# The order of latent and context columns at the two norms of a two-model Trainium2 kernel

## What is computed

```python
def _layer(x, ctx, ..., update_ctx):            # second model, called for l = 0 and l = 1
    hx = _rmsnorm(x, norm_g) * (1.0 + scale_x) + shift_x
    hc = _rmsnorm(ctx, norm_g) * (1.0 + scale_c) + shift_c
    px = hx @ w_in
    a_k, a_v, b_k, b_v, a_q, b_q, a_z, b_z, g_a, g_b = _split(px, SPLIT_SIZES)
    pc = hc @ (w_in if update_ctx else w_in[:, :KV_COLS])
    ...
    x_new = x + gate_x * out_x
    if update_ctx:                              # only for l = 0
        ctx = ctx + gate_c * out_c
    return x_new, ctx
```

## Time and profile before

| | |
|---|---|
| median of 3 runs | 2992.94 us (2992.8 to 2994.6) |
| the profiled execution: its time, its span | 2993.36 us, 2991.7 us |
| TensorE busy | 2904.7 us, 97% of the span |
| VectorE, ScalarE, GpSimd busy | 1041.1, 720.0, 232.8 us |
| TensorE's mean granted clock | 0.989 |

### The profile page before, as it was taken

One profiled execution on the slowest core, in us unless ns is written; L12 is line 12 of the kernel. 1 busy time (PEld: TensorE's weight loads), 2 busy tenths in 40 slices (PEclk: granted clock), 3 DMA queues, 4 the chain that ended last, 5 costly groups with the idle time before them and its releaser, 6 DMA issues.

```text
span 2991.7 us, 41281 instructions
## 1 busy us (share of the span) xinstructions
PE 2904.7 (97%) x16802; PEld 1686.2 (56%) x16802; DVE 1041.1 (35%) x2032; ACT 720.0 (24%) x1389; POOL 232.8 (8%) x296
## 2 busy tenths in 40 slices
PE   6899999999999999999998999999999899999998
PEld 2777777776444444444444567765555544775443
DVE  3455555553231234444312226521011312552011
ACT  3344444442200002212002226620000012462000
POOL 0222222220000000000000101000000001100000
PEclk9999999999999999999999999999999999999999
DMA  5111111103244433444321210001111122101222
GB/s 204 54 40 40 35 41 35 35 30 128 77 141 139 136 97 126 161 147 155 98 84 58 74 43 30 1 29 56 50 49 49 49 63 75 43 2 57 77 76 72
DMA packets 61301, 220.93 MB, mean 74 GB/s; under 512 B 6688, under 2 KB 8864, under 8 KB 60896
## 3 DMA queue, kind: packets, MB, share of 16 engines
q1 hardware_dynamic: 42512, 153.11, 16.2%
q0 software_dynamic: 14656, 56.93, 5.9%
q10 hardware_dynamic: 3984, 8.71, 0.8%
HBM read 215.01 MB, written 2.15 MB: 73 GB/s over the span
## 4 chain that ended last, share of the span: by engine, by line
PE 95%; DMA 1%; DVE 1%; ACT 1%; issue 1%; POOL 0%; DVEq 0%; ACTq 0%; POOLq 0%; SPq 0%
PE psum L366 92%; PE psum L735 3%; DMA arena<-in_ctxT 1%; DMA arena<-in_stream 0%; DMA arena<-in_mods 0%; PE psum L552 0%; DVE arena L1258 0%; ACT arena L923 0%; ACT arena L1043 0%; PE psum L505 0%; ACT arena L1146 0%; ACT arena L916 0%; DVE arena L1636 0%; ACT arena L910 0%; DVE arena L1650 0%
## 5 line engine op out<-in xcount | busy, mean ns | idle before, releaser
L366 PE MATMUL psum<-arena 64*64 64x64 f32 (+6 forms) x16002 | 2810.6, 359 | 74.2 <-ACT arena L923 15.7
L366 PEld LDWEIGHTS psum<-arena 128*128 128x128 f32 (+4 forms) x16002 | 1599.9, 161 | 1266.5 <-issue 1114.5
L1477 DVE SCALAR_TENSOR_TENSOR arena<-arena 128x1024 f32<-128x1024 f32 x128 | 149.2, 1220 | 5.1 <-DMA arena<-in_mods 4.8
L1730 DVE SCALAR_TENSOR_TENSOR arena<-arena,psum 128x512 f32<-128x512 f32 x32 | 21.2, 684 | 371.7 <-PE psum L366 371.7
L1146 ACT ACTIVATE arena<-psum,arena 128x512 f32<-128x512 f32 (+2 forms) x160 | 115.3, 728 | 31.2 <-DVE arena L1642 18.2
L1200 ACT ACTIVATE arena<-psum 128x512 f32<-128x512 f32 x32 | 19.1, 597 | 372.5 <-PE psum L366 372.5
L1604 DVE COPY arena<-psum 128x512 f32<-128x512 f32 x26 | 18.0, 692 | 238.8 <-PE psum L366 238.8
L735 PE MATMUL psum<-arena 128*128 128x128 f32 x704 | 94.2, 279 | 4.2 <-ACT arena L1146 4.0
L1821 POOL DMA_DIRECT2D arena<-in_bias x16 | 8.8, 552 | 1111.6 <-DVE arena L1614 849.6
L735 PEld LDWEIGHTS psum<-arena 128*128 128x128 f32 x704 | 76.3, 140 | 29.0 <-issue 14.8
L1815 POOL DMA_DIRECT2D arena<-in_mods x76 | 40.1, 528 | 670.0 <-DVE arena L1477 670.0
(11 more groups left out here) (206 smaller groups left out, 1340.5 us busy)
## 6 DMA issues: line engine op xcount, KB each, us to landing
arena<-in_stream SPq DMA_DIRECT2D x288, 512.0 KB, 3.6
arena<-in_mods POOLq DMA_DIRECT2D x80, 512.0 KB, 3.6
arena<-gc_rows POOLq DMA_DIRECT2D x16, 384.0 KB, 4.7
arena<-in_bias POOLq DMA_DIRECT2D x16, 384.0 KB, 3.9
arena<-in_xT ACTq DMA_DIRECT2D x1, 2048.0 KB, 18.2
out<-arena SPq DMA_DIRECT2D x1, 2048.0 KB, 7.2
arena<-in_conds ACTq DMA_DIRECT2D x1, 1536.0 KB
arena<-arena POOLq DMA_DIRECT2D x4, 384.0 KB, 4.3
```

The source lines that it names most:

```text
L366: return pe.matmul(out, lhsT, rhs, start=start, stop=stop, skip_group_check=True)
L1477: m = stt(mjunk[:, b % 2, :] if x < len(conds) - 1 else slot, slot, 0.5, cb[:, c, :], ALU.mult, ALU.mult, accum_out=dst(x))
```

## The change

Norm 2 and norm 4 are each split in two, the context's part ("2c", "4c") ahead of the latent's.

- The context's sum is a small product of its own (`ctx_norm_sum`, into bank 1). At layer 0 it stands in the middle of the down product, after its fourth output tile; at layer 1 in the middle of the last output tile of the out product, whose context products now come before its latent ones (this order holds for output tiles 3 and 7). VectorE scales the context's eight tiles before it adds the last latent tile.
- The value product is done in two passes over the same four weight tiles. The first does the two context chunks for all eight k, with the latent's sum after k = 2 (into bank 0); the second does the four latent chunks for all eight k. The context chunks stand in banks 2 and 3 and the latent chunks in 4 to 7 (`value_bank`). A weight tile counts as used after the second pass.
- Five loops of two rounds over the output tiles are written out as straight code (down product and out product on TensorE, their additions on VectorE), and the wait for `con2` stands behind the value product.

```diff
+ROOTS = {n: at + 1 for at, n in enumerate((0, 1, "2c", 2, 3, "4c", 4))}
+NORMED = {n: KT * at for at, n in enumerate((0, 1, "2c", 2, "4c", 4))}
...
+        def value_bank(c):
+
+            return 4 + c if c < XC else 2 + c - XC
+
...
+            def ctx_norm_sum(count):
+
+                pe.wait_ge(s("sqsum"), count)
+                mm(psum[:, 1, 0:CTX], ones, sqb[:, 1, SEQ:TOK]).then_inc(s("nsum"), 1)
+
...
-            with pe.Fori(0, 2) as i:
+            for i in range(2):
                 for j in range(4):
                     pe.wait_ge(s("xd"), 4 * i + j - 3 + 4)
                     for b in range(3):
                         kt = 8 if b < 2 else FT - 16
                         product(T_DOWN + 3 * j + b, G, 4 + j, None, i, 12, kt, 8 * b, b == 0, b == 2)
-            norm_sums(2, (0, 1), True)
+                if i == 0:
+                    ctx_norm_sum(SUMS[2] - KT)
...
+                def near_values(k, chunks, normed):
+
+                    w = weights(pe, T0 + L_VA + k // 2)
+                    pe.wait_ge(s("H"), normed + k + 1)
+                    for c in chunks:
+                        m = mm(psum[:, value_bank(c), :], H[:, k, c * P:(c + 1) * P],
+                               w[:, (k % 2) * NAW:(k % 2 + 1) * NAW], k == 0, k == KT - 1)
+                    if k % 2 and c < XC:
+                        m.then_inc(s("used"), 1)
+
+                for k in range(KT):
+                    near_values(k, range(XC, CH), NORMED["4c" if l else "2c"])
+                    if k == 2:
+                        pe.wait_ge(s("sqsum"), SUMS[4] + 1 if l else SUMS[2])
+                        mm(psum[:, 0, :], ones, sqb[:, 1, 0:SEQ]).then_inc(s("nsum"), 1)
+                for k in range(KT):
+                    near_values(k, range(XC), NORMED[4 if l else 2])
                 pe.wait_ge(s("b2load"), 16 * 2)
-                if l:
-                    norm_sums(4, (0, 1), True)
-                for q in range(4):
-                    w = weights(pe, T0 + L_VA + q)
-                    for kk in range(2):
-                        k = 2 * q + kk
-                        pe.wait_ge(s("H"), KT * (2 + l) + k + 1)
-                        for c in range(CH):
-                            m = mm(psum[:, 2 + c, :], H[:, k, c * P:(c + 1) * P], w[:, kk * NAW:(kk + 1) * NAW],
-                                   k == 0, k == KT - 1)
-                    m.then_inc(s("used"), 1)
...
+                        w = weights(pe, T0 + L_OUT + j, i, 4)
+                        for k in range(KT):
+                            m = mm(psum[:, slot2(j)[1], 0:CTX], w[:, k * P:(k + 1) * P], MG2[:, k, SEQ:TOK],
+                                   k == 0, k == KT - 1)
+                        m.then_inc(s("out_ctx"), 1)
+                        for k in range(KT):
+                            m = mm(psum[:, slot2(j)[0], 0:SEQ], w[:, k * P:(k + 1) * P], MG2[:, k, 0:SEQ],
+                                   k == 0, k == KT - 1)
+                            if i and k == 2:
+                                ctx_norm_sum(SUMS[4])
+                        m.then_inc(s("used"), 1)
...
+            norm_root("2c", ((SEQ, TOK, 1),))
+            norm_shift(NORMED["2c"], ((SEQ, TOK, 1),), adaT[:, 0:8, :])
             act.wait_ge(s("xd"), 8 + 4)
             act.dma_start(con2, a_con2).then_inc(s("b2load"), 16)
-            norm_root(2, (0, 1), True, eps=vec("eps", 5))
+            norm_root(2, ((0, SEQ, 0),), eps=vec("eps", 5))
...
+                    norm_root("4c", ((SEQ, TOK, 1),))
+                    norm_shift(NORMED["4c"], ((SEQ, TOK, 1),), adaT[:, 24:32, :])
+                    norm_root(4, ((0, SEQ, 0),))
+                norm_shift(NORMED[4 if l else 2], ((0, SEQ, 0),), adaT[:, 24 * l:24 * l + 8, :])
...
+                if i == 0:
+                    dve.wait_ge(s("gmod"), 4)
+                    norm_scale("2c", ((SEQ, TOK, 1),))
...
+                    for k in range(KT - 1):
+                        dve.wait_ge(s("used"), T0 + L_OUT + k + 1)
+                        for q in range(2):
+                            add_out(k, q)
+                        dve.wait_ge(s("b2_xo"), 2 * k + 2 + 8)
+                        squares_add(4, k, TOK)
+                    dve.wait_ge(s("out_ctx"), 2)
+                    add_out(KT - 1, 1)
+                    last_squares(1, SEQ, TOK)
+                    norm_scale("4c", ((SEQ, TOK, 1),))
+                    dve.wait_ge(s("used"), T0 + L_OUT + KT)
+                    add_out(KT - 1, 0)
+                    last_squares(2, 0, SEQ)
```

More of the change, by code:

```diff
@@ L891, in _ @@
                 pe.wait_ge(s("b2_tg"), 16 * l + 2 * KT + FREE)
-                with pe.Fori(0, 2) as i:
+                for i in range(2):
                     for j in range(4):
                         pe.wait_ge(s("b2_xo"), 16 * l + (2 - l) * (4 * i + j - 3) + 8)
-                        product(T0 + L_OUT + j, MG2, *(slot2(j) if wide else (slot2(j)[0], None)), i, 4,
-                                ready=None if j else ("b2_mg", 8 * l + FREE))
+                        if not wide or j < 3:
+                            product(T0 + L_OUT + j, MG2, *(slot2(j) if wide else (slot2(j)[0], None)), i, 4,
+                                    ready=None if j else ("b2_mg", 8 * l + FREE))
+                            continue
+                        w = weights(pe, T0 + L_OUT + j, i, 4)
[9 more added lines that the diff above has]
+                        m.then_inc(s("used"), 1)
         @block.scalar
@@ L905, in _, with norm_root @@
             f = act.activation
-            def norm_root(n, banks, wide, eps=vec("eps"), ctx_eps=vec("eps"), to=rnorm):
+            def norm_root(n, parts, eps=vec("eps"), to=rnorm):
                 act.preload_act_table_set("natural_log_exp_and_others")
[L909 to L912, removed]
+                act.wait_ge(s("nsum"), ROOTS[n])
+                for a, b, bank in parts:
+                    m = f(to[:, a:b], psum[:, bank, 0:b - a], ACT.Ln, bias=eps, scale=1.0 / D)
                 m.then_inc(s("nln"), 1)
-                act.wait_ge(s("nln"), n + 1)
-                w = TOK if wide else SEQ
-                f(to[:, 0:w], to[:, 0:w], ACT.Exp, scale=-0.5).then_inc(s("rnorm"), 1)
+                act.wait_ge(s("nln"), ROOTS[n])
+                a = parts[0][0]
+                f(to[:, a:b], to[:, a:b], ACT.Exp, scale=-0.5).then_inc(s("rnorm"), 1)
             def norm_shift(h0, parts, shift):
@@ L1226, in squares_begin @@
                 if n:
-                    dve.wait_ge(s("rnorm"), n)
+                    dve.wait_ge(s("rnorm"), ROOTS[3 if n == 4 else n - 1])
                 dve.memset(sqb[:, 1, :], 0.0).then_inc(s("sqsum"), 1)
@@ L1254, in norm_scale @@
                         h, x, r = H[:, k, a:b], X[:, k, a:b], rnorm[:, a:b]
-                        if n >= 2 and not a:
+                        if n in (2, 4):
                             h = h.rearrange("p (c r) -> p c r", r=ROWS)
@@ L1585, in _ @@
             dve.wait_ge(s("gate"), 4)
-            with dve.Fori(0, 2) as i:
+            for i in range(2):
                 for j in range(4):
```

60 lines of the change are left out of this document (27 added, 33 removed).

## The result

| | changed kernel | kernel before | ratio, 95% interval |
|---|---|---|---|
| first set | 2966.11 us (2964.47 to 2968.45, 4 runs) | 2992.87 us (4 runs) | 0.9910 [0.9893, 0.9927] |
| second set (`again`) | 2968.11 us (2965.89 to 2969.21, 5 runs) | 2991.56 us (15 runs) | 0.9919 [0.9905, 0.9932] |
| third set (`again2`) | 2965.10 us (2961.33 to 2969.30, 4 runs) | 2992.98 us (7 runs) | 0.9899 [0.9882, 0.9915] |

The change takes off 26.8, 23.5 and 27.9 us, 0.8 to 1.0%. `again` and `again2` are the same changed kernel, run again beside the experiments. The profiled execution took 2968.45 us (span 2966.8 us), against 2993.36 us: 24.9 us less.

A forecast was written before the change was run, and what follows sets the result against it. TensorE, busy for 97% of the span, was taken as the bound. Filling its holes and slow starts would save 10.9 us at norm 2 and 13.2 at norm 4, 24.1 in all, giving 2969.0 us, range 2966 to 2975.

The forecast's parts named there:

- The two terms of the sum: From the down or out product's end to the value product's copy: 10.9 us less at norm 2, 13.2 at norm 4.
- The margins: Time to spare before TensorE would wait at the two norms; tightest 0.8 us, at the context's sum of norm 4.
- the term "nothing": Outside the two norms: weight tiles, PSUM banks and written-out loops were taken to change the time by nothing.
- the lower bound of 2966: Low end of the range, allowing half-clock stretches elsewhere to shift by part of one, worth 2.2 to 2.9 us.
- On TensorE they don't show: Register instructions saved by written-out loops: no gain on TensorE, as 352 records with one loop back ran without a hole.
- theory B: Theory put to the experiments: some 2 us of the gain are the change's own, from the written-out loops.
- The gaps filled as worked out: Main case, both norms: the holes are filled as calculated, 2966 to 2971.5 us; chance 0.79.
- hand-over at norm 4: Rival, VectorE between output tile 6 and the context's scale: 3 us later than said, giving 2975 us; chance 0.08.
- the clock did not fall where there was no hole: Rival, behind the norms: half clock has another cause than idle time, 5.6 us stay, giving 2974.6 us; chance 0.06.
- given back: Rival, behind the value product: a later stage with its own pace leaves the end at 2993 us; chance 0.03.
- the ring: Rival, four weight-tile slots: the query product's first tiles come too late at both layers, giving 3000 us; chance 0.03.
- fetch of 3.3 us: Rival, TensorE's three loops back: each hid an instruction fetch, so 9.9 us more would go, giving 2959 us; chance 0.01.

The follow-up runs named there:

- loops_only: Kernel before with the loops written out, plus only the changed bank numbers and the place of the context's gain: 2988.87 us, ratio 0.9990.
- fill_before: Kernel before with products of 256 columns that nobody reads put into TensorE's holes at norms 2 and 4: 2988.96 us, single execution.
- one_pass: Changed kernel with the context's norm still early, but the value product in one pass behind the latent's sum: 2985.20 us, single execution.
- sum_k0: Changed kernel with the latent's sum behind k = 0 of the first pass instead of k = 2: 2970.22 us, single execution.
- norm2_only: Kernel before with the written-out loops and the split and two passes at norm 2 only: 2979.30 us, ratio 0.9956.
- norm4_only: Kernel before with the written-out loops and the split and two passes at norm 4 only: 2979.73 us, ratio 0.9960.
- sum_last: Changed kernel with the latent's sum behind k = 7, at the end of the first pass: 2976.91 us, single execution.
- fill_all: Changed kernel with unread products in further waits: first model's merge, norm 1's sum, first transposes of each attention: 2963.01 us, 0.9894 of before.

## Why the prediction was nearly right, and what it missed

**The two terms of the sum.** Norm 2: 10.9 us said, 10.87 measured. Norm 4: 13.2 said, 13.24 measured. The copy starts 1622.02 - (1427.81 + 151.63 + 0.43) = 42.15 us after the down product, and 2411.91 - 2369.79 = 42.12 us after the out product; I had said 42.1.

**The margins.** All held, with more room than said: context sum at norm 4 1.2 us instead of 0.8, first context `H` 2.4 instead of 1.9, latent squares 2.9 instead of 1.4. Squares of 256 columns took 0.42 and 0.43 us, as taken. The eight scalings of 256 columns took 3.26 us, not 3.8, so VectorE was free for the last latent addition at 2369.71 and not 0.7 us late.

**The step that failed is the term "nothing" for what lies outside the two norms.** The first set gave 26.8 us, and 2.7 us of it are not in my 24.1, nor in the 24.11 that the two norms measure. I took the difference of two kernels for the difference of two norms, with the rest of the program the same. In the profiles the rest holds two terms that I had at nothing: 1.71 us because the clock fell behind a 1.97 us hole at the first attention in the profile of before and not in that of the changed kernel, and 0.5 us in all from the written-out loops. I knew of such stretches and put them into the range, but as if they could only shift, not fail to come (the lower bound of 2966 is built on that, and the first set used up all of it); and I read one profile of before as if every execution had its stretches. In the experiments the fall at that place is in `loops_only`, `fill_before`, `one_pass` and `sum_k0`, and not in `again`, `again2`, `norm2_only`, `norm4_only` and `sum_last` (`fill_all` has products in the hole). `loops_only` and `norm4_only` are the same program up to there, and the clock fell in one and not in the other; so the change is not needed for it to stay up. At layer 1's attention, behind a hole of 2.02 us, it fell in `norm4_only`, `fill_before`, `sum_k0` and `sum_last`, which is why their E - V1 is 1.3 to 1.6 us longer, and not in before, nor in the changed kernel's three profiles. Whether the change moves the odds is not shown: at layer 0 the clock fell in one of six profiles with two passes at norm 2 and in four of five without, at layer 1 in three of six with two passes at norm 4 and in one of five without.

**The written-out loops.** "On TensorE they don't show" held for the loop back, but not for the way into the loop, 0.27 us ahead of the down product: I read only the inside of that row. And I looked at no other engine. On VectorE the loop cost 0.23 to 0.25 us at each hand-over from TensorE, and at norm 2 idle times of 0.23 and 0.15 us further on. These shorten the old holes by 0.55 and 0.41 us. In the changed kernel they lie under products and only widen the margins, but for the last addition of the program.

**What stays open.** The profiles of before and of the changed kernel are accounted for: 24.9 us are 24.11 of the two norms, 1.71 of the attention's clock and 0.23 of the last addition, less 1.14 by which the changed kernel came to D later. The medians are not. `loops_only` measured 2.7 us below before, with an interval from 0.3 to 5.7 us; the profiles show some 1.0 us of that as the loops' (0.27 ahead of D, 0.5 at norm 4 by `norm2_only`, 0.23 at the end, nothing clear at norm 2). With the loops' 0.5 us the changed kernel should give 24.6 us, and how often the clock falls at the attention in executions without a profile is not known. The three sets gave 26.8, 23.5 and 27.9. So of theory B 0.5 us are shown, and its 2 us are not excluded. What is above 24.6 us in the first and third set is put down to chance of the clock, at the attention and ahead of D, where the same code comes up to 5.7 us sooner or later; that is argued and not shown.

**The rivals.** The gaps filled as worked out was the case. No hand-over at norm 4 was late, the clock did not fall where there was no hole, E - V1 is the same within 0.3 us so nothing was given back, TensorE's row at both places runs on into the query product so the ring was in time, and no loop hid a fetch of 3.3 us: what a loop cost TensorE is the 0.27 us ahead of D.

## What to carry to other kernels

Where a chain of small steps stands between two products and part of the next product doesn't need it, do that part over the chain: count the idle time and also the half clock behind it, which here made a hole of 3.4 us cost 5.3 to 6.6. Measure a stage between two instructions that both kernels have; where no clock fell it repeated within 0.02 us over the three profiles of the changed kernel, while whole executions differed by several. Before you take "nothing" for the rest of the program, look for holes at which the clock sometimes falls, and price them on both sides.

## What the runs showed of the hardware

- TensorE's clock after one and the same hole is not always the same. Behind 1.96 us at the attention it fell to 1.2 GHz in some executions and stayed at 2.4 GHz in others, with a difference of 1.57 us in the next 24 records and 1.6 to 1.7 us in all. D, behind the same code in all kernels but `fill_all` (save the 0.27 us at the loop), comes between 1422.95 (`sum_last`) and 1428.67 us (`again2`), so 5.7 us of an execution's time are settled before the change begins.
- Products whose result nobody reads hold the clock up in a wait. In `fill_before` idle times of 0.31 to 0.56 us were left, and the granted clock was 1.00.
- Going into a loop on TensorE that waits for another engine took 0.27 us longer than straight code here: the down product began 0.33 us after VectorE's releasing instruction had ended (1425.65 + 0.69 us), and 0.06 us after it (1427.06 + 0.69) with the loop written out.
- In a loop on VectorE with addresses made from the loop's counter, an addition started 0.27 to 0.29 us after TensorE's last record, and idle times of 0.23 and 0.15 us stood between dependent instructions at norm 2; written out, all three were 0.04 us. Register instructions alone don't explain it: one stands ahead of L1237 at norm 4 too, which started 0.04 us after L1235.
